# State-space decays from a table of running sums, and the group norm's root by Newton steps on four columns

## The reference, cut to what matters

```
a_cs  = cumsum(dt * a) inside a chunk                # per head, dt > 0, a < 0
decay = exp(where(l >= s, a_cs[l] - a_cs[s], -inf))  # 128 x 128 per chunk and head
y_diag = (C B^T * decay) (x dt)
states = B^T (exp(a_cs[last] - a_cs) x dt), carried over chunks by exp(a_cs[last])
y_off  = (C prev_state) * exp(a_cs)
y = (y_diag + y_off + d_skip x) * silu(z)
y = y * rsqrt(mean(y*y over the group's 256 channels) + 1e-6) * g_ssm_norm
```

## Time and profile before

| | |
|---|---|
| median of 3 runs | 1365.37 us (1363.85 to 1366.72) |
| the profiled execution | 1366.59 us, its span 1364.8 |
| TensorE, VectorE, ScalarE, GpSimd busy | 1311.0, 682.9, 560.1, 525.6 us |
| chain that ended last | TensorE 81%, VectorE 7%, ScalarE 6%, issue 4% |
| group loop, per round | dtab copy 0.94 us, ScalarE table loads 4 of 1.28 us, y_hi and y_lo 1.3 each |
| granted TensorE clock | 0.99 over the span |

### The profile page before, as it was taken

How to read it: one execution, slowest core, us unless ns; L and a number is a source line. 1 busy time by engine, 2 the same in 40 slices (tenths; PEclk the granted TensorE clock), 3 DMA queues, 4 the chain that set the end, 5 groups by cost and what they waited for, 6 DMA issues and landing times.

```text
span 1364.8 us, 19170 instructions
## 1 busy us (share of the span) xinstructions
PE 1311.0 (96%) x6848; PEld 1061.8 (78%) x6848; DVE 682.9 (50%) x1020; ACT 560.1 (41%) x977; POOL 525.6 (39%) x317
## 2 busy tenths in 40 slices
PE   7999979999999999999999999999999999999997
PEld 5788756767688887888787788888878888888886
DVE  5745566666558778877885212111145043151433
ACT  5324345556545455546554422222353232242233
POOL 2432334444433323333332344444434444444442
PEclk9999989999999999999999999999999999999999
DMA  8423310000022222222222333333423332332332
GB/s 249 123 62 62 77 47 1 2 1 1 1 78 63 63 76 77 61 65 73 77 61 66 87 94 93 98 102 92 170 78 94 106 94 92 96 104 92 92 103 97
DMA packets 174708, 108.20 MB, mean 79 GB/s; under 512 B 20963, under 2 KB 162499, under 8 KB 174659
## 3 DMA queue, kind: packets, MB, share of 16 engines
q1 hardware_dynamic: 174658, 107.54, 27.7%
HBM read 105.43 MB, written 2.10 MB: 79 GB/s over the span
## 4 chain that ended last, share of the span: by engine, by line
PE 81%; DVE 7%; ACT 6%; issue 4%; POOL 1%; SPq 0%; DMA 0%; DVEq 0%; ACTq 0%
PE bank L1922 19%; PE bank L1573 14%; PE bank L1936 10%; PE bank L1926 9%; PE bank L1577 7%; PE bank L1942 5%; PE bank L1782 3%; PE bank L1730 2%; PE bank L1765 2%; PE bank L1901 1%; PE bank L1854 1%; PE bank L1633 1%; PE bank L1907 1%; PE bank L1824 1%; DVE grp L1395 1%
## 5 line engine op out<-in xcount | busy, mean ns | idle before, releaser
L654 POOL TENSOR_TENSOR wlo<-raw,whi 128x1024 fp32r<-128x1024 f32 x182 | 448.0, 2462 | 717.6 <-ACT whi L861 592.4
L861 ACT ACTIVATE whi<-raw 128x1024 fp32r<-128x1024 f32 x158 | 167.4, 1060 | 569.9 <-PE bank L1926 269.7
L1573 PE MATMUL bank<-h_hi,whi 128*128 128x512 f32 x560 | 228.5, 408 | 7.6 <-issue 2.9
L1573 PE MATMUL bank<-h_lo,whi 128*128 128x512 f32 x560 | 219.4, 392 | 0.0
L1922 PE MATMUL bank<-h_hi,whi 128*128 128x512 f32 x384 | 150.3, 391 | 1.4 <-DVEq L1464 0.9
L1922 PE MATMUL bank<-h_lo,whi 128*128 128x512 f32 x384 | 149.4, 389 | 0.0
L1577 PE MATMUL bank<-h_hi,wlo 128*128 128x512 f32 x560 | 138.3, 389 | 0.0
L1573 PEld LDWEIGHTS bank<-h_hi,whi 128*128 128x128 f32 x560 | 105.9, 189 | 36.0 <-issue 10.1
L1531 DVE TENSOR_TENSOR uf<-rel 128x512 f32<-128x512 f32 x32 | 80.3, 2509 | 90.8 <-ACT rel L1019 90.8
L1573 PEld LDWEIGHTS bank<-h_lo,whi 128*128 128x128 f32 x560 | 105.8, 189 | 23.8 <-issue 3.1
L1577 PEld LDWEIGHTS bank<-h_hi,wlo 128*128 128x128 f32 x560 | 105.1, 188 | 21.9
(11 more groups left out here) (258 smaller groups left out, 2167.7 us busy)
## 6 DMA issues: line engine op xcount, KB each, us to landing
raw<-in_w_in SPq DMA_DIRECT2D x78, 512.0 KB, 3.8
raw<-in_w_up SPq DMA_DIRECT2D x32, 512.0 KB, 4.0
raw<-in_w_down SPq DMA_DIRECT2D x32, 512.0 KB, 3.7
raw<-in_w_ssm_branch SPq DMA_DIRECT2D x16, 512.0 KB, 3.7
raw<-in_w_in SPq DMA_DIRECT2D x16, 256.0 KB, 3.8
raw<-in_w_attn_branch SPq DMA_DIRECT2D x8, 512.0 KB, 3.6
raw<-in_w_o SPq DMA_DIRECT2D x8, 512.0 KB, 3.7
x_sb<-in_x SPq DMA_DIRECT2D x4, 512.0 KB, 5.8
```

What stands on the lines that cost most here:

```text
L654: nc.gpsimd.tensor_tensor(wlo[slot][:], raw[slot][:], whi[slot][:].bitcast(F32), ALU.subtract).then_inc(wlo_ready, 1)
L861: nc.scalar.activation(whi[slot][:], raw[slot][:], ACT.Copy).then_inc(whi_ready, 1)
L1573: T.matmul(bank[slot][:], whi[slot][:, k * P:(k + 1) * P], part[:, k, :], start=(k == 0 and n == 0), stop=False)
```

## The change

- K/V stage: after the dt values are turned, VectorE writes -dt a twice, side by side, into a padded tile (`dta_wide`), TensorE multiplies it with the triangle (4 f32 matmuls of 128 columns, after unit 10), and VectorE makes from the result a table `decay_rows`: rows 64 to 95 hold the running sums of the 32 heads in fp32r, rows 96 to 127 the rest, rows 0 to 63 ones. `pick` chooses a head's rows. The former split of dt a (4 instructions at L1169 to L1173, less the first) goes.
- In a group `seg_heads_now` writes the lower half of two `picked` tiles, `seg_operand(c)` is one product over 64 partitions that reads partitions 64 to 127 and writes 0 to 63, and `seg(c)` is one matmul. Its result is a_cs[l] - a_cs[s] for all l and s; `seg_exp` clips it at 0 with a Relu of the negated value and takes Exp with scale -1. Its places on ScalarE move one step earlier.
- The eo sums become two fp32r matmuls of 384 columns with `pick_wide` (VectorE, 128 x 256) and the table.
- The group norm: VectorE adds the two squares (`sum_squares`), TensorE makes four one-column matmuls into 4 columns of bank 5, VectorE takes the root of 128 x 4 numbers by a seed and three Newton steps (11 instructions, each waiting for the one before), TensorE spreads the columns over 128 rows by four f32 matmuls (`norm_spread`, after unit 3), and `normed_y` reads that bank. ScalarE's `norm_root` goes. On VectorE `normed_y` moves behind conv 3, `low_y` behind `mdec`; on ScalarE `high_y` moves behind the first Silu of z. C B^T waits for normed_y, since it writes the same bank.
- Last group: the same steps with bank 6; the spread stands inside product 2 of the first mix tile.

```diff
@@ ScalarE
-            def norm_root(g, sums=2):
-                act.wait_ge(yms_done, g + 1)
-                nc.scalar.activation(rs, bank[sums][:], ACT.Ln, bias=eps_col[:, 0:1]).then_inc(yln_ready, 1)
...
-                    nc.scalar.activation(mdec[:, c].rearrange("p h l -> p (h l)"), bank[6 + c % 2][:],
-                                         ACT.Exp).then_inc(dec_exp, 1)
+                    fall = mdec[:, c].rearrange("p h l -> p (h l)")
+                    nc.scalar.activation(fall, bank[6 + c % 2][:], ACT.Relu, scale=-1.0).then_inc(dec_read, 1)
+                    act.wait_ge(dec_read, g * 4 + (c + 1))
+                    nc.scalar.activation(fall, fall, ACT.Exp, scale=-1.0).then_inc(dec_exp, 1)
...
                 conv_first(0)
+                seg_exp(0)
                 for j in range(1, 4):
                     arrive(j)
                     conv_first(j)
-                    seg_exp(j - 1)
...
+                    seg_exp(j)
+                    if j == 1 and not first:
                         squares(g - 1)
-                    elif j == 2:
-                        norm_root(g - 1)
-                    else:
-                        high_y(g - 1)
-                seg_exp(3)
                 for j in range(4):
                     conv_silu(j)
                 arrive(4)
                 nc.scalar.activation(grp[:, 4, :], bank[0][:], ACT.Silu).then_inc(unit_read[0], 1)
+                if not first:
+                    high_y(g - 1)
@@ VectorE, K/V stage
+                    V.memset(dta_wide[:, :, 0:HD], 0.0).then_inc(dta_spread, 1)
+                    for part in range(2):
+                        V.tensor_scalar(dta_wide[:, :, HD + HEADS * part:HD + HEADS * (part + 1)], dtT[:, 1], -1.0, None,
+                                        ALU.mult).then_inc(dta_spread, 1)
...
                 if j == 10:
+                    dve.wait_ge(decay_summed, 1)
+                    lower = slice(HD + HEADS, P)
+                    V.tensor_copy(decay_rows[0:HD, :].rearrange("p (c l) -> p c l", c=NC),
+                                  ones[0:HD, :].unsqueeze(1).to_broadcast([HD, NC, P])).then_inc(decay_split, 1)
+                    V.tensor_copy(decay_rows[HD:HD + HEADS, :], bank[2][HD:HD + HEADS, :]).then_inc(decay_split, 1)
+                    V.tensor_copy(decay_hi[lower, :], bank[2][lower, :]).then_inc(decay_split, 1)
+                    dve.wait_ge(decay_split, 3)
+                    V.tensor_tensor(decay_rows[lower, :], bank[2][lower, :], decay_hi[lower, :].bitcast(F32),
+                                    ALU.subtract).then_inc(decay_split, 1)
                     dve.wait_ge(hid_ready, 2)
@@ VectorE, groups
-            def normed_y(g):
+            def norm_root(g, sums=5):
+                mean, part, corr = (bank[sums][:, i * NC:(i + 1) * NC] for i in range(3))
+                dve.wait_ge(yms_done, g + 1)
...
+                root_step(V.tensor_scalar(mean, mean, EPS, None, ALU.add))
+                root_step.wait()
+                root_step(V.tensor_scalar(root[:].bitcast(I32), mean.bitcast(I32), -0.5, ROOT_SEED, ALU.mult, ALU.add))
+                for again in range(3):
+                    root_step.wait()
+                    root_step(V.tensor_tensor(part, mean, root[:], ALU.mult))
+                    root_step.wait()
+                    root_step(V.scalar_tensor_tensor(corr, part, -0.5, root[:], ALU.mult, ALU.mult))
+                    root_step.wait()
+                    ins = V.scalar_tensor_tensor(root[:], corr, 1.5, root[:], ALU.add, ALU.mult)
...
+            def sum_squares(g):
+                dve.wait_ge(ysq_ready, g * 2 + 2)
+                V.tensor_tensor(sq[:, 0, :], sq[:, 0, :], sq[:, 1, :], ALU.add).then_inc(sq_summed, 1)
...
+                def seg_heads_now():
+                    if not first:
+                        dve.wait_ge(seg_summed, g * 4)
+                    for to in picked:
+                        V.tensor_scalar(to[HD:P], pick[HD:P, heads].unsqueeze(2).to_broadcast([HD, HPG, P]), -1.0, None,
+                                        ALU.mult).then_inc(seg_heads, 1)
                 def seg_operand(c):
-                    if c or not first:
-                        dve.wait_ge(seg_summed, g * 4 + c)
-                    for part, to in enumerate((seg_hi, seg_lo)):
-                        V.tensor_tensor(to[:], tri.unsqueeze(1).to_broadcast([P, HPG, P]),
-                                        dta_parts[:, part, c, heads].bitcast(F32).unsqueeze(2).to_broadcast([P, HPG, P]),
-                                        ALU.mult).then_inc(segr_ready, 1)
+                    if c >= 2:
+                        dve.wait_ge(seg_summed, g * 4 + (c - 1))
+                    V.tensor_tensor(picked[c % 2][0:HD],
+                                    decay_rows[HD:P, c * P:(c + 1) * P].bitcast(F32).unsqueeze(1).to_broadcast([HD, HPG, P]),
+                                    pick[HD:P, heads].unsqueeze(2).to_broadcast([HD, HPG, P]),
+                                    ALU.mult).then_inc(segr_ready, 1)
...
+                seg_heads_now()
                 seg_operand(0)
                 seg_operand(1)
                 conv(0)
...
                 seg_operand(3)
+                if not first:
+                    sum_squares(g - 1)
+                if not first:
+                    dve.wait_ge(eo_summed, g * 2)
+                V.tensor_copy(pick_wide[:], pick[:, heads].unsqueeze(2).to_broadcast([P, HPG, HD])).then_inc(pick_ready, 1)
+                if not first:
+                    norm_root(g - 1)
                 conv(2)
+                conv(3)
                 if not first:
                     normed_y(g - 1)
-                conv(3)
-                if not first:
-                    low_y(g - 1)
@@ TensorE
-                for j in range(2):
-                    pe.wait_ge(ysq_ready, g * 2 + (j + 1))
-                    mm = T.matmul(bank[sums][:], mean_ssm[:], sq[:, j, :], start=(j == 0), stop=(j == 1))
+                pe.wait_ge(sq_summed, g + 1)
+                pe.wait_ge(y_gated, g * 2 + 2)
+                for c in range(NC):
+                    mm = T.matmul(bank[sums][:, c:c + 1], sq[:, 0, c * P:(c + 1) * P], mean_ssm[:, 0:1], start=True, stop=True)
                 mm.then_inc(yms_done, 1)
+            def norm_spread(g, spread=5):
+                pe.wait_ge(yrs_ready, g + 1)
+                for c in range(NC):
+                    mm = T.matmul(bank[spread][:, c * P:(c + 1) * P], root[:, c:c + 1].to_broadcast([P, P]), ident,
+                                  start=True, stop=True)
+                mm.then_inc(yrs_spread, 1)
...
-                    for part in (seg_hi, seg_lo):
-                        mm = T.matmul(bank[6 + c % 2][:], stri_r[:], part[:].rearrange("p h l -> p (h l)"),
-                                      start=(part is seg_hi), stop=(part is seg_lo))
+                    T.matmul(bank[6 + c % 2][:], decay_rows[:, c * P:(c + 1) * P], picked[c % 2][:].rearrange("p h l -> p (h l)"),
+                             start=True, stop=True).then_inc(seg_summed, 1)
...
                 pe.wait_ge(conv_ready, g * 4 + 4)
+                if not first:
+                    pe.wait_ge(yn_ready, g * 2)
...
-                    for c in range(1, NC):
-                        mm = T.matmul(bank[6 + j][:, c * P:(c + 1) * P], dtab[:, c - 1, j * P:(j + 1) * P], tri,
-                                      start=True, stop=True)
+                    T.matmul(bank[6 + j][:, P:S], pick_wide[:, 2 * j:2 * j + 2].rearrange("p h d -> p (h d)"),
+                             decay_rows[:, P:S], start=True, stop=True).then_inc(eo_summed, 1)
```

More of the change, by code:

```diff
@@ L77 @@
 MAGIC = 12582912.0
+ROOT_SEED = 1597463007.0
 TWO_PI = 2 * np.pi
@@ L270, in build @@
         cbm = sb("cbm", [P, NC, P])
-        seg_hi = sb("seg_hi", [P, HPG, P], F32R)
-        seg_lo = sb("seg_lo", [P, HPG, P], F32R)
+        picked = [sb(f"picked{i}", [P, HPG, P], F32R) for i in range(2)]
         mdec = sb("mdec", [P, NC, HPG, P])
         prev = sb("prev", [P, NC - 1, HPG * HD])
-        dtab = sb("dtab", [P, NC - 1, HPG * HD])
+        pick_wide = sb("pick_wide", [P, HPG, HD], F32R)
+        at[0] = max(at[0], after_y + 2 * 4 * KT * S + 2 * 2 * 4 * S)
         yt = sb("yt", [P, 2, S])
@@ L1182, in _ @@
                                       ).then_inc(kvc_ready, 1)
-                if j == 10:
+                if j == 8:
+                    V.memset(dta_wide[:, :, 0:HD], 0.0).then_inc(dta_spread, 1)
+                    for part in range(2):
+                        V.tensor_scalar(dta_wide[:, :, HD + HEADS * part:HD + HEADS * (part + 1)], dtT[:, 1], -1.0, None,
+                                        ALU.mult).then_inc(dta_spread, 1)
+                    step(V.tensor_scalar(pick[0:HD, :], ident[0:HD, 0:HEADS], 0.0, None, ALU.mult))
+                    for part in range(2):
+                        rows = slice(HD + HEADS * part, HD + HEADS * (part + 1))
```

(27 more changed lines are left out.)

62 lines of the change are left out of this document (33 added, 29 removed).

## The result

The changed kernel takes 1386.69 us (median of 4 runs, 1377.86 to 1391.61) against 1366.02 (1363.85 to 1366.72) for the kernel before beside it: a ratio of 1.014 [1.0114, 1.0166]. It is 1.4% slower. The forecast was 1348.0, the range 1341 to 1364: wrong, on the wrong side. What came true is rival A. Ratios further on are against the kernel before run beside each version; among its runs beside the last four versions are two of 2630 and 4587 us, slow ones that no ratio uses.

A forecast was written before the change was run, and what follows sets the result against it. TensorE, busy 96% of the span, was taken as the bound. Rounds -15.5, group 0 -2.0, K/V stage +0.9 and +0.3, before the mix +1.1, mix -2.2 sum to -17.4 us: 1348.0 against the median 1365.37, range 1341 to 1364.

The forecast's parts named there:

- rival A: Group loop: GpSimd's weight split takes the shared SBUF port before seg operand 2; 1378, or 1390 with halved clock; chance 0.18.
- All this hidden work costs nothing as long as seg operand 2 is on time: Group loop: VectorE's and ScalarE's work stays hidden behind TensorE, adding only a 0.25 us wait for the squares' sum.
- from about 0.1 us: Shared port in the group loop: the start difference from which the order of seg operand 2 and GpSimd's split decides.
- rows 13: Profile rows cited against the port loss: VectorE's L1259 starts 0.13 us after GpSimd's L669 yet takes its usual 0.41.
- The price of a lost round: Group loop: TensorE waits 4.6 us instead of 0.25, 4.3 more a round; a halved clock adds 1.7.
- The rest of the sum: Forecast terms besides the port: seven rounds -15.5, group 0 -2.0, K/V stage +0.9 and +0.3, mix +1.1 and -2.2 us.
- Rival B's first leg: Root on VectorE: steps take 0.4 us, unit 4 0.5 late each round, 3.5 lost; whole rival 1352 to 1360, chance 0.12.
- The idle before the transposes: TensorE in each round: 0.66 us idle before L1874, forecast to shrink by 0.65 us.
- no load in ScalarE between tap 2 and Silu: Sign of being right: ScalarE's group-loop timeline shows no table load between those two steps.
- Rival B's third leg: ScalarE: Relu and Exp need different tables, two 1.28 us loads in each of 4 pairs, 11 lost; whole rival 0.12.
- rival B's second leg: norm_sum on TensorE: one-column matmuls cost as much as 512 columns, +0.8 a round, 5.7 lost; whole rival 0.12.
- The tail: End of the kernel: +1.1 us idle before the mix, then -2.2 in it, unit 4 ending at 764.8 instead of 767.0.

The follow-up runs named there:

- decay: The changed kernel with only its decay part, the group norm left as in the kernel before: 1356.7 us, ratio 0.9928 to the kernel before.
- pesum: The changed kernel with the squares summed by TensorE, eight one-column matmuls for four and no VectorE sum: 1360.09 us, ratio 0.9945 to the kernel before.
- late16: The changed kernel with a 16-column memset on VectorE just before seg operand 2 in rounds 1 to 7: median 1395.88 us.
- early: The changed kernel with seg operand 2 moved ahead of conv 0 on VectorE: 1352.48 us, ratio 0.9894 to the kernel before.
- norm: The changed kernel with only its norm part, the decays left as in the kernel before: 1412.61 us, ratio 1.0342 to the kernel before.

## Why the prediction was wrong

**The step that failed** is "All this hidden work costs nothing as long as seg operand 2 is on time", with rival A at 0.18: the sum put the lost port at nothing, and it cost 38.8 us in five of seven rounds. Its arithmetic was good: it put the two starts 0.02 us apart, with VectorE later, and they are 0.003 to 0.031 apart, with VectorE later. Its mechanism was good as well: it had the sum of squares end at 17.2 on its clock after a lost race, and it ended 17.1 after (488.44, with zero at 471.38). What failed is the weight. I set against A that L1259 was served although it started 0.13 us after GpSimd's L669, and took from it that a little later doesn't lose. That GpSimd instruction is of another kind (512 columns, one tensor and pointer scalars), and the case did not carry over. The same pair of instructions as in the race stood in the trace as well: seg_lo and the split, with seg_lo 0.28 behind and held for 2.2 us, and 0.17 behind and held again in each round's second stall. That row bore on the race more closely than L1259. Against the split the edge is sharp: over the changed kernel, decay, pesum and late16, all 22 rounds with VectorE 6 ns or more behind are lost, and all 6 with it 2 to 4 ns behind are won. Nor is it "from about 0.1 us". Why L669 yielded was not tried. It was no accident of one row: another product of two tiles in SBUF that starts 0.06 us behind the second L669 of that pair takes 0.46 us and so is hardly held either (timeline of the kernel before), and both L669 take 1.0 us instead of 0.77.

```profile
202.58 0.46 DVE L1268 TENSOR_TENSOR cp<-cp,cst 128x256 f32<-128x256 f32 x1
```

The Trainium skill ("SBUF — State Buffer", Who interferes with whom) has whoever issues first hold the shared pair for the whole instruction, with the other fully blocked. For the operand and the split the runs agree, 2.94 against 0.69 us and 2.97 against 2.41, up to the 4 ns by which a winner may start later in the records. For L669, taken at the records' word, they don't. I had named that rule and the outcome it gives, and let one row of another instruction outweigh it. With a tie forecast to 0.02 us, A deserved about half of the chance, whatever rows 13 show.

**The price of a lost round** was put at 4.3 us for the wait, which is the 4.28 above. The clock was put at 1.7; it took 3.69 there, and in the rounds of 50.7 the rest of 7.5, 3.2. With five of seven lost instead of all, the errors largely cancel, so it is partly luck that 1386.69 lies inside rival A's 1378 to 1390: A had every round lost, and nothing in it foresaw that rounds of one execution would differ. At 7.5 to 8.0 us a round the spread of 14 us between the runs would be two rounds more or fewer; that is an estimate, since only one of them has a profile.

**The rest of the sum**, read from the won rounds and from early, stands. By stretches of the changed kernel's span: up to the first eo 413.96, forecast 412.9 (the kernel before at 412.65, less the 0.9 of group 0's seg, plus the 1.2 of the K/V stage); a round 43.22, forecast 43.1; from the last round's end 634.1, forecast 633.0. (The sum's 7 x 2.2 is 15.4 and not 15.5, and its round from 503 to 549 us is the third of the seven; neither matters.)
- The root's steps take 2.2 us (536.56 to 538.74), spaced 0.20 us, where 0.24 was taken; those that write into PSUM take 0.17 us and those that write into SBUF 0.16. Rival B's first leg falls.
- The idle before the transposes is gone: the product at 546.77 runs into L1944 at 548.59.
- One load of tables (1.28) stands between the last tap and Silu, as the prediction's own clock had it (its sign of being right, "no load in ScalarE between tap 2 and Silu", did not fit that clock), and none between Relu and Exp. Rival B's third leg falls.
- The one-column matmuls cost as much as those of 128 columns: their passes start 0.11 us apart, and the next unit starts 0.91 behind the first of them (a row is 1.05 us long, as the spread's is). The 0.90 taken was right, its lower end 0.47 not, and rival B's second leg falls.

The beginning is 1.0 late. TensorE's wait for hidr is 0.53 where 0.3 was taken. Its waits for the positions' DMA and for h_lo are 1.5 and 2.0 where they were 0.3 and 0.5 before, which is more than the 1.0, so something else came out shorter; it was not traced. In early, with the same code there, the two are 0.7 and 0.5, so they belong to the execution rather than to the change.

**The tail** is 1.1 longer than the forecast. The order of waits was as predicted, 1.87 us before the mix and 1.34 for the sum, but the clock fell behind the second and not behind the first, where the prediction, outside its sum, had priced it at 1.7 (TensorE of the changed kernel, chain of waits and timeline):

```profile
757.80 3.91 PE bank L1993 x16
...
771.65 1.02 PE bank L1895 x8
772.67 3.98 PE bank L1993 x10
```
```profile
773.59 0.63 PE L1993 MATMUL bank<-o_lo,whi 128*128 128x512 f32 x1
774.02 0.63 PE L1993 MATMUL bank<-o_hi,whi 128*128 128x512 f32 x1
```

Ten products take 3.98 us there where sixteen take 3.91: 1.7 lost, less the 0.5 of waiting for the root, which did not come. The stall at 759.81 of the kernel before is gone. In early, behind the same wait of 1.9 us before the mix, the clock did fall, and the same sixteen products take 5.47 us (early's chain of waits):

```profile
719.58 5.47 PE bank L1993 x16
```

## What to carry to other kernels

Before work that TensorE will wait for is put on VectorE's queue, look at what already stands ahead of it there: a port stall that costs next to nothing today is paid in full from then on. Where two engines that share a port come out of the sum within some hundredths of a microsecond of each other, each round can fall either way; compute the time of both outcomes, and reorder so that the shared-port instruction lies a whole instruction ahead. The cure cost nothing here: one line moved, 34 us. And look at each part of a change alone: here the new norm gives only 0.6 us a round once nothing waits.

## What the hardware showed beyond what was expected

- The order on the shared pair turns within a few nanoseconds of the records (won at 2 to 4 ns behind, lost from 6), so that the seven rounds of one execution, with the same instructions, fall either way: 43.2 or 51.2 us.
- After a wait of 4.4 us TensorE ran at 1.2 GHz for 6.8 to 10.2 us in the five lost rounds of the changed kernel, but for only 3.4 us in four of norm's seven, after the same wait. Idle length alone does not foretell it. In the changed kernel the clock stays full after the 1.87 us at 757.80 and is halved after the 1.34 us at 771.65; in early it is halved after both. And the wait of 2.58 us for y_lo, behind which the kernel before falls to half clock, stands in decay as well, where the clock stays full.
- A f32 matmul with one moving column costs 0.11 us a pass, as one with 128 columns does (0.89 in the chain for 8 at 542.37). The loads of its 128 by 128 stationary tile take 0.97 us for the 8, the same pace, so that they may be what bounds it; no run varies them.
